# Second sequence of an encoder block: expert row sums issued between the eight parts of its inverse transform, and its first spectrum load moved up in the load queue

## What is computed

```python
def bidirectional_fftconv(z, kf, kb):
    k = concatenate([kf.at[0].add(kb[0]), zeros, kb[1:][::-1]])
    return irfft(rfft(z, n=2 * L) * rfft(k), n=2 * L)[:, :L]
def encoder_layer(x, ...):
    a, hy, gates = split(rmsnorm(x) @ w_in)
    ya = multiscale_pool(a) @ w_pool_out
    yb = hyena_mixer(hy) @ w_hyena_out
    h = x + (sigmoid(gate_a) * ya + sigmoid(gate_b) * yb) @ w_o
    return h + peer(rmsnorm(h))
def peer_block(xb, ...):        # 128 tokens
    act = gelu(einsum('ted,td->te', u_tab[idx], xb)) * gate      # idx: T x 128 experts
    return einsum('te,ted->td', act, v_tab[idx])
```

## Time and profile before

| | |
|---|---|
| Median of the 3 runs shown | 3088.54 us (3088.43 to 3096.27) |
| The profiled execution | 3098.64 us, of it the span 3096.5 us |
| Share of the span busy: PE, PEld, DVE, ACT, POOL | 86%, 53%, 73%, 34%, 33% |
| DMA | 998.59 MB, mean 322 GB/s |
| Mean granted TensorE clock | 0.945 of full |
| Chain of waits that ended last, by engine | DMA 31%, DVE 21%, PE 14%, issue 10%, ACT 4% |

### The profile page before, as it was taken

The page is one execution under the profiler, slowest core; times in us unless marked ns, Lnnn a source line. Parts: engine busy times, 40 slices in busy tenths (PEclk is TensorE's granted clock), DMA queues, the critical chain, the costliest instruction groups (busy, mean ns, idle before and its releaser), DMA issues.

```text
span 3096.5 us, 29223 instructions
## 1 busy us (share of the span) xinstructions
PE 2665.9 (86%) x9109; PEld 1641.0 (53%) x9109; DVE 2274.0 (73%) x4295; ACT 1063.2 (34%) x2757; POOL 1021.7 (33%) x694
## 2 busy tenths in 40 slices
PE   6999999687789998789766998899899989899993
PEld 4556647433334444355344665666666666666661
DVE  5341124786799677687886899988889998888888
ACT  4211122221234885378574222223222223222221
POOL 2111212142344322233222443433344443334333
PEclk9999999899899999899888999999999999999997
DMA  4332245397899989889799999999999999999996
GB/s 153 110 103 69 92 172 182 127 389 259 328 354 382 340 318 355 361 336 341 290 383 344 404 401 405 387 409 409 412 398 397 404 379 410 397 406 409 410 412 263
DMA packets 246384, 998.59 MB, mean 322 GB/s; under 512 B 20855, under 2 KB 99447, under 8 KB 161752
## 3 DMA queue, kind: packets, MB, share of 16 engines
q0 software_dynamic: 92160, 671.13, 54.6%
q1 hardware_dynamic: 152344, 300.45, 26.9%
q10 hardware_dynamic: 1728, 25.17, 2.0%
HBM read 950.26 MB, written 46.40 MB: 322 GB/s over the span
## 4 chain that ended last, share of the span: by engine, by line
DMA 31%; DVE 21%; PE 14%; issue 10%; ACT 4%; SPq 1%; POOL 0%; DVEq 0%; ACTq 0%; POOLq 0%
DMA row<-in_peer_uv,row_u 26%; DVE h_tile L1806 8%; DVE row L1795 4%; PE job_ps L689 3%; PE job_ps L1551 3%; DMA arena<-in_peer_ut 2%; PE wide_ps L689 2%; PE job_ps L1526 1%; DVE uw_lo L1815 1%; DMA hand<-in_w_o 1%; PE wide_ps L1526 1%; DMA arena<-in_inv_cnt 1%; DVE arena L1826 1%; ACT arena L1632 1%; DVE prod L233 1%
## 5 line engine op out<-in xcount | busy, mean ns | idle before, releaser
L1495 POOL DMA_INDIRECT row<-in_peer_uv,row_u x640 | 903.7, 1412 | 1566.1 <-DVE h_tile L1806 1202.7
L1795 DVE CUSTOM_DVE_ANT_0 row<-row,x_tile 128x1024 f32<-128x1024 f32 x640 | 780.5, 1221 | 256.3 <-DMA row<-in_peer_uv,row_u 253.2
L1564 PE MATMUL job_ps<-arena 128*128 128x512 f32 x1536 | 683.5, 595 | 10.9 <-DVE arena L1826 10.9
L1806 DVE SCALAR_TENSOR_TENSOR h_tile<-row,act_e,h_tile 128x1024 f32<-128x1024 f32 x512 | 654.0, 1277 | 1.5 <-ACT act_e L1683 0.9
L1679 ACT ACTIVATE gelu_e<-dots 128x1 f32<-128x1 f32 x640 | 128.5, 201 | 1392.6 <-DVE dots L1795 1390.8
L128 PE MATMUL wide_ps<-x_hi,uw_lo 128*128 128x384 f32 x1024 | 380.4, 371 | 125.4 <-DVE uw_lo L1815 124.8
L1564 PEld LDWEIGHTS job_ps<-arena 128*128 128x128 f32 x1536 | 289.8, 190 | 321.8 <-issue 308.0
L130 PE MATMUL wide_ps<-x_hi,uw_hi 128*128 128x384 f32 x1024 | 355.3, 347 | 0.0
L129 PE MATMUL wide_ps<-x_lo,uw_hi 128*128 128x384 f32 x1024 | 354.3, 346 | 0.0
L1551 PE MATMUL job_ps<-row,diag 128*128 128x512 f32 x512 | 262.4, 641 | 59.4 <-ACT diag L1690 59.4
L128 PEld LDWEIGHTS wide_ps<-x_hi,uw_lo 128*128 128x128 f32 x1024 | 201.2, 196 | 208.3 <-DVE uw_lo L1815 202.1
(11 more groups left out here) (252 smaller groups left out, 3005.9 us busy)
## 6 DMA issues: line engine op xcount, KB each, us to landing
arena<-in_peer_ut SPq DMA_DIRECT2D x128, 512.0 KB, 14.0
arena<-in_peer_v SPq DMA_DIRECT2D x128, 512.0 KB, 12.6
hand<-tmp_gates SPq DMA_DIRECT2D x32, 768.0 KB, 18.4
tmp_gates<-arena ACTq DMA_DIRECT2D x10, 2048.0 KB, 11.8
arena<-in_w_in SPq DMA_DIRECT2D x32, 512.0 KB, 3.5
hand<-in_w_in SPq DMA_DIRECT2D x32, 512.0 KB, 7.0
row<-in_peer_uv,row_u POOLq DMA_INDIRECT x640, 9.8
arena<-in_x SPq DMA_DIRECT2D x16, 512.0 KB, 6.0
```

What stands on the lines that cost most here:

```text
L1495: pool.indirect_dma_start(row[n % NR][:], None, dram["peer_uv"], bass.IndirectOffsetOnAxis(row_u[g % 2][:, e:e + 1], 0)).then_inc(row_in[n ...
L1564: last = pe.matmul(job_ps[q][:], actd[j % 2][:, d * P:(d + 1) * P], vw[j % NO][:, half * 512:(half + 1) * 512], start=j == 0, stop=j == P - 1)
L1795: dve.tensor_tensor_reduce(out=mine, in0=mine, in1=xb[g % 2][:], scale=1.0, scalar=0.0, op0=ALU.mult, op1=ALU.add, accum_out=dots[:, n % N ...
L1806: dve.scalar_tensor_tensor(out=side, in0=row[n % NR][:, D:2 * D], scalar=act_e[:, n % NA:n % NA + 1], in1=side, op0=ALU.mult, op1=ALU.add) ...
```

## The change

Two edits. Ahead of parts 1 to 7 of the inverse transform TensorE's generator now yields a due time, an eighth of the unit apart, if the sequence is the second. By the due times above the parts then stand at steps 37, 38, 39, 41, 42, 44, 45, 47, and what is due in between stands between them: `sum_row(37)` (step 40) after the third part, `sum_row(41)` (step 44) after the fifth. `sum_row(45)` (step 48) and all that follows stay behind the eighth. And `load_spectrum(0)` moves from behind the loads after `z` 7 to behind the weight load after `z` 4, ahead of the weight loads after `z` 5, 6 and 7 and of the four tables. No computation is added or removed; the first sequence's instructions are untouched.

```diff
                 while ci < {"z": 4, "f": n + 5, "i": len(self.consts)}[kind]:
                     self.load_const(sp, ci)
                     ci += 1
-                if self.kf is not None and kind != "i" and (kind == "z" or n % 2 == 0 and n < 6):
-                    self.load_spectrum(sp, 0 if kind == "z" else n // 2 + 1)
+                if self.kf is not None and kind == "f" and n % 2 == 0 and n < 6:
+                    self.load_spectrum(sp, n // 2 + 1)
+            if (kind, n) == ("z", 2 * CT - 4) and self.kf is not None:
+                self.load_spectrum(sp, 0)
...
                 for e, k in enumerate(DFT_ORDER):
                     ci = self.consts.index(("i", k))
+                    if self.ready and e:
+                        yield self.begin[kind, n] + e / 8 * (self.end[kind, n] - self.begin[kind, n])
                     pe.wait_ge(self.y_done, e + 1)
                     pe.wait_ge(self.c_in[ci % 4], 16 * (ci // 4 + 1))
                     for c in range(CT):
```

## The result

The changed kernel took 3068.68 us (median of 4 runs, 3062.88 to 3072.71), the kernel before 3089.43 us beside it: a ratio of 0.9924, 95% interval 0.9896 to 0.9952. Twelve more runs later in the study gave 3071.22 against 3089.64 us, 0.9939 (0.9919 to 0.9959). The predicted 3068.5 us and its range hold. Whether each term of the sum holds is another question, and one of them does not. One execution of the kernel before, in the series of e9 to e12, took 4571 us at a mean granted clock of 0.557; the ratios leave it out, and the median of 3090.05 us further down counts it.

The account below looks back on a forecast made before the run. The prediction took stalls between coupled engines, with no engine full, to bound the kernel from 697 to 820 us. Terms 6 - 1 + 15.2 + 2 - 2 = 20 us off 3088.54 us gave 3068.5 us, range 3059 to 3081.

Parts of the forecast that it names:

- each term of the sum: Gains in us: spectrum stall 6, early load -1, row sum 15.2, `inv_cnt` for pooling 2, less DMA room -2.
- one of them: Term for the spectrum stall ahead of the first products: loading the first spectrum earlier gains 6 us (0 to 9.7).
- a row sum: Row sum of row 37 behind the inverse transform: moving it between parts brings row 43 15.2 us sooner (13 to 16).
- The other stall: VectorE's 12.22 us wait for the first spectrum, `tmp_kf`: it goes, and the first product starts 11.4 us earlier.
- the turn-taking by packets: DMA engines serve queues a packet at a time, so short-row tables beside gathers land slowly: 28.7 us against 8.0.
- a full path: Memory-bound rival, 697 to 820 us: late rows leave 8 of the 20 us gained, 3080.5 us; chance 0.12.

Follow-up runs that it names:

- e9: Against the kernel before, only the first spectrum load moved earlier, the inverse transform left in one piece: 3089.58 us against 3090.05, ratio 0.9993.
- e12: The kernel before with 4 MB of extra HBM-to-HBM copies in the second sequence: 3092.48 us, ratio 1.0011.
- e6: The changed kernel with the first spectrum load later, behind the fifth table: 3072.75 us, ratio 0.9921 to the kernel before.
- e5: The changed kernel with the transform's first six parts together, row sums 37 and 41 behind them: 3081.72 us, ratio 0.9954 to the kernel before.

## What to carry over

When engines share a ring of buffers, look for the instruction that frees the buffer and for what stands ahead of it in its engine's list: here a row sum stood behind 29 us of other matmuls, VectorE lost 16 us by it, and a due time between the parts gave back these and some 20 us in time. The other stall had 12 us in the trace and no gain in the medians of 24 executions, so a stall's length in the trace is not yet its price. A stretch in which the DMA engines run dry (88 GB/s against 384) may be the sign that tells them apart; one case of each does not prove it. Two traces of one kernel say how large a difference may be before it is believed; timing each edit alone says whose it is.

## What was unexpected in the hardware

- 256 KB loads in 512-byte rows, four issued together beside the gathers, took up to 28.7 us (25.4 in e6, 21.6 in e5), and SP was held for 11.4 us at the transfers behind them; in 2 KB rows they took 14.0 us at most. That agrees with the turn-taking by packets that the prediction quoted from the Trainium skill, page "DMA: Bandwidth & Descriptors", section "Queues, rings and completion order"; but no row of the experts came clearly sooner by it.
- A DMA share of 97% did not mean a full path: with 4 MB more the same rows ran at 386 GB/s instead of 357.
- The traces differ in three places, whatever the kernel: row 0 came 599.7 to 610.6 us from the start, and rows 96 to 192 took 396.8 to 408.3 us. Rows 192 to 639 took 1696.4 to 1700.0 us in ten of fourteen traces and 1703 to 1708 in the other four.
